# Spreading two gate rows to 128 partitions: diagonals and matmuls with ones, or a trip through memory

## What is computed

```python
mod = c_act @ w_mod[l] + b_mod[l]
sh1, sc1, g1, sh2, sc2, g2 = [m[:, None, :] for m in jnp.split(mod, 6, axis=-1)]
h = rms_norm_2(x, norm_attn[l]) * (1.0 + sc1) + sh1
qa, ka, va, qb, ckv, qi, ki, wi = jnp.split(h @ w_in[l], SPLIT_POINTS, axis=-1)
...
mix = jnp.concatenate([out_a, out_b], axis=-1) @ w_out[l]
x = x + g1 * mix
h = rms_norm_2(x, norm_ffn[l]) * (1.0 + sc2) + sh2
x = x + g2 * conv_ffn(h, w_up[l], conv_w[l], conv_b[l], w_down[l])
```

## Time and profile before

| | us |
|---|---|
| median of 3 runs | 2412.99 |
| lowest and highest | 2411.38, 2413.26 |
| profiled execution | 2410.21 |
| its span | 2408.5 |

### The profile page before, as it was taken

How to read it: one execution, slowest core, us unless ns; L and a number is a source line. 1 busy time by engine, 2 the same in 40 slices (tenths; PEclk the granted TensorE clock), 3 DMA queues, 4 the chain that set the end, 5 groups by cost and what they waited for, 6 DMA issues and landing times.

```text
span 2408.5 us, 29108 instructions
## 1 busy us (share of the span) xinstructions
PE 2294.6 (95%) x10764; PEld 1888.7 (78%) x10764; DVE 1672.4 (69%) x1848; ACT 991.6 (41%) x1009; POOL 133.3 (6%) x190
## 2 busy tenths in 40 slices
PE   8799998989999999999879999998999999999996
PEld 7688886878888878788668677877788888888885
DVE  6688787787776867767683556785466666666666
ACT  4543443433443334334333345434444444444442
POOL 2011000000000000000000000000000000000000
PEclk9899998999999999999988999999999999999998
DMA  8678675777877777777535444454555555555552
GB/s 290 233 260 271 228 265 188 256 268 250 289 237 255 274 248 264 258 259 273 199 108 134 149 117 132 140 181 156 175 185 185 188 192 186 181 190 191 181 189 101
DMA packets 261800, 501.28 MB, mean 208 GB/s; under 512 B 16753, under 2 KB 70289, under 8 KB 261104
## 3 DMA queue, kind: packets, MB, share of 16 engines
q1 hardware_dynamic: 230656, 382.39, 48.1%
q0 software_dynamic: 30800, 117.03, 14.0%
q10 hardware_dynamic: 288, 1.11, 0.1%
HBM read 496.80 MB, written 3.67 MB: 208 GB/s over the span
## 4 chain that ended last, share of the span: by engine, by line
PE 54%; issue 36%; DVE 4%; DMA 4%; ACT 2%; POOL 1%; SPq 0%; DVEq 0%; ACTq 0%; POOLq 0%
PE pair_t L399 15%; PE pair_t L401 15%; PE pair_t L400 15%; DMA raw<-in_attn_w_in_dram 1%; PE turn L507 1%; PE sc L1501 1%; DVE m_acc L980 1%; ACT w_hi L388 1%; DVE w_lo L393 1%; PE sc L737 1%; PE sc L514 1%; DMA raw<-in_ret_w_out_dram 1%; DMA raw<-in_w_in_dram 1%; PE sc L729 1%; PE turn L1509 0%
## 5 line engine op out<-in xcount | busy, mean ns | idle before, releaser
L393 DVE TENSOR_TENSOR w_lo<-raw,w_hi 128x2048 fp32r<-128x2048 f32 (+1 forms) x371 | 824.5, 2225 | 566.6 <-ACT w_hi L388 561.3
L388 ACT ACTIVATE w_hi<-raw 128x2048 fp32r<-128x2048 f32 (+1 forms) x371 | 690.9, 1864 | 1095.2 <-DMA raw<-in_ret_w_in_dram 367.0
L399 PE MATMUL pair_t<-w_hi,x_hi 128*128 128x512 f32 (+2 forms) x2112 | 825.0, 391 | 19.5 <-DVE w_lo L393 16.4
L401 PE MATMUL pair_t<-w_hi,x_lo 128*128 128x512 f32 (+2 forms) x2112 | 811.1, 384 | 0.0
L400 PE MATMUL pair_t<-w_lo,x_hi 128*128 128x512 f32 (+2 forms) x2112 | 810.6, 384 | 0.0
L399 PEld LDWEIGHTS pair_t<-w_hi,x_hi 128*128 128x128 f32 x2112 | 402.0, 190 | 106.2 <-DVE w_lo L393 17.8
L401 PEld LDWEIGHTS pair_t<-w_hi,x_lo 128*128 128x128 f32 x2112 | 401.6, 190 | 78.0
L400 PEld LDWEIGHTS pair_t<-w_lo,x_hi 128*128 128x128 f32 x2112 | 402.1, 190 | 73.7 <-issue 0.2
L980 DVE SCALAR_TENSOR_TENSOR m_acc<-m_raw,csilu,m_acc 128x1024 f32<-128x1024 f32 x180 | 230.7, 1281 | 4.3 <-DMA m_raw<-in_w_mod_dram 0.9
L399 PE MATMUL pair_t<-w_hi,f_hh 128*128 128x512 f32 x352 | 140.4, 399 | 6.9 <-DVE f_hl L2243 6.9
L401 PE MATMUL pair_t<-w_hi,f_hl 128*128 128x512 f32 x352 | 138.6, 394 | 0.0
(11 more groups left out here) (332 smaller groups left out, 2073.5 us busy)
## 6 DMA issues: line engine op xcount, KB each, us to landing
m_raw<-in_w_mod_dram POOLq DMA_DIRECT2D x96, 1024.0 KB, 6.9
raw<-in_ret_w_in_dram SPq DMA_DIRECT2D x192, 512.0 KB, 4.6
raw<-in_w_up_dram SPq DMA_DIRECT2D x176, 512.0 KB, 4.2
raw<-in_w_down_dram SPq DMA_DIRECT2D x88, 512.0 KB, 4.4
raw<-in_attn_w_in_dram SPq DMA_DIRECT2D x64, 512.0 KB, 4.6
raw<-in_ret_w_out_dram SPq DMA_DIRECT2D x64, 512.0 KB, 4.6
raw<-in_w_in_dram SPq DMA_DIRECT2D x56, 512.0 KB, 4.6
raw<-in_attn_w_out_dram SPq DMA_DIRECT2D x32, 512.0 KB, 4.9
```

The source lines that it names most:

```text
L388: act.activation(chunk(w_hi, c, width), chunk(raw, c, width), ACT.Copy).then_inc(sem("hi"), 1)
L393: v.tensor_tensor(chunk(w_lo, c, width), chunk(raw, c, width), chunk(w_hi, c, width).bitcast(F32), ALU.subtract).then_inc(sem("lo"), 1)
L399: pe.matmul(to, xh, wh, start=start, stop=False)
L401: return pe.matmul(to, xl, wh, start=False, stop=stop)
```

## The change

The 8 diagonals, the 32 matmuls with ones and the 8 copies go. After chunk 1 of block 1 PE transposes the 16 columns of g1 and the 16 of g2 into bank `sc[1]`: 16 partitions, 256 columns. DVE copies them to `gate_rows` after its second chunk of block 2. POOL writes them to a scratch tensor in memory, 2 x 2048 values, waits for the write, and issues two loads that read one row of 2048 values each and write it to all 128 partitions of `rows`. POOL does this behind the loads of `b_wuk` and `b_wuv`, ahead of the latent's power. DVE waits for `gate_out` ahead of the first head's scores, since `gate_rows` shares their buffer, and for `gate_in` ahead of the first sum. PE's wait for the eight copies becomes a wait for the one, a chunk later.

```diff
-        gate_diag = over("gate_diag", b_s_at, [2, 4, P], F32)
+        gate_rows = over("gate_rows", b_s_at, [2 * P], F32)
...
+        gates = nc.dram_tensor("gate_rows_kept", (2, D), F32, kind="Internal").ap()
...
-            def gates(c):
-                for b in range(2):
-                    n = 2 * c + b
-                    if n == 0:
-                        pe.wait_ge(sem("mod_read"), A_KV + R_HEADS)
-                    pe.wait_ge(sem("gate_diag"), n + 1)
-                    if n >= 2:
-                        pe.wait_ge(sem("gate_row"), n - 1)
-                    for m in range(4):
-                        mm = pe.matmul(sc[b][:, m * P:(m + 1) * P], ones[:, :], gate_diag[:, b, m, :],
-                                       start=True, stop=True)
-                    mm.then_inc(sem("gate_mm"), 1)
             def turn_qi0(c):
                 if c == 0:
                     pe.wait_ge(sem("i_q"), 1)
                     pe_turn_pairs(pe, i_q, "i_q_turned")
-                gates(c)
+                elif c == 1:
+                    pe.wait_ge(sem("mod_read"), A_KV + R_HEADS)
+                    for m in range(2):
+                        mm = pe.transpose(sc[1][0:KC, m * P:(m + 1) * P],
+                                          modc[:, (2 + 3 * m) * KC:(3 + 3 * m) * KC], ident[:, :])
+                    mm.then_inc(sem("gate_turned"), 1)
...
-                    pe.wait_ge(sem("gate_row"), 8)
...
+                    pe.wait_ge(sem("gate_copied"), 1)
...
-            act_blocks(act, B_B0 + 1, {0: [lambda: qi(0), lambda: qiT(0), lambda: gates(0)],
-                                       **{c: [lambda c=c: gates(c)] for c in (1, 2, 3)}})
+            act_blocks(act, B_B0 + 1, {0: [lambda: qi(0), lambda: qiT(0)]})
...
+            def gates_copied():
+                v.wait_ge(sem("gate_turned"), 1)
+                v.tensor_copy(gate_rows[0:KC, :], sc[1][0:KC, 0:2 * P]).then_inc(sem("gate_copied"), 1)
...
-            vec_blocks(v, B_B0 + 1, {0: [lambda: mod_read(v, A_KV + R_HEADS - 1), lambda: gates(0)],
-                                     1: [lambda: qiT(0), lambda: gates(1)],
-                                     2: [lambda: gates(2)], 3: [lambda: gates(3)]})
+            vec_blocks(v, B_B0 + 1, {0: [lambda: mod_read(v, A_KV + R_HEADS - 1)],
+                                     1: [lambda: qiT(0)], 2: [gates_copied]})
...
+                    if g == 0:
+                        v.wait_ge(sem("gate_out"), 16)
...
+                if t == 0 and c == 0:
+                    v.wait_ge(sem("gate_in"), 16 * 2)
...
+            g.wait_ge(sem("gate_copied"), 1)
+            get(bass.AP(tensor=gates.tensor, offset=gates.offset, ap=[[P, KC], [D, 2], [1, P]]),
+                gview(gate_rows[0:KC, :], 2), "gate_out")
+            g.wait_ge(sem("gate_out"), 16)
+            for m in range(2):
+                get(rows[:, m, :], broadcast_row(gates, m * D, D), "gate_in")
```

More of the change, by code:

```diff
@@ L1789, in done @@
                 act.wait_ge(sem("products"), CH * (B_B0 + b) + 4)
[L1791 to L1796, removed]
             act_blocks(act, B_B0, {})
```

## The result

| | before | changed |
|---|---|---|
| median, us | 2412.18 (4 launches) | 2397.61 (4 launches) |
| lowest and highest | 2410.98, 2413.26 | 2393.91, 2398.79 |
| profiled execution | 2410.21 | 2398.79 |
| ratio, 95% interval | | 0.9939, 0.9923 to 0.9956 |

What follows compares the result with a forecast made beforehand. PE's own order was taken to bound the kernel; savings after block 1's four chunks, 3.0 + 3.3 + 1.7 + 1.7 = 9.7 us, took the median from 2412.99 to 2403.3 us, range 2397.5 to 2407.2.

Steps and rivals of the forecast that it cites:

- The pieces: Gate matmuls after each of the four chunks of block 1, second attention; removing them saves PE 9.7 us net.
- The share of the waits: PE's idle time ahead of gate pieces in block 1, 2.6 us of the 9.7 forecast.
- The transposes: Two transposes with 128 columns added on PE after chunk 1 of block 1; taken as 0.3 us, no wait.
- ACT, DVE, POOL, the trip: Removed copies and diagonals give nothing beyond the waits; added DVE copy, POOL's write and two row loads cost 0.
- The cover: Rows' 2.1 MB beside blocks 2 and 3's loads: 8.9 us free against 6.5 needed; block 2's last small chunk ready in time.
- Block 2's clock: Block 2's 96 matmuls keep their two speeds, 17.58 us in all; bounds 10.8 and 20.5 us.
- The critical load: Last chunk of block 3, loaded once block 2 releases its buffer; moves with block 2's end and keeps its 5.40 us.
- The starting point: Median of the runs of the kernel before, 2412.99 us; runs spread over 1.9 us, 1 us allowed either way.
- B: Rival, 12%: clock stays high through block 2; 2398.5 us, or 2396.6 if no queue forms.
- B's second half: With block 2 fast, DMA becomes the bound, last landing at 1308.9; only 4.8 of the 6.7 us count.
- C: Rival, 12%: clock falls at block 2's first narrow matmul (2.9 us) or rows jam (2.2 us); 2406.2 us.
- D: Rival, 3%: row loads served slowly, wait after block 2 grows; slower by 4.8 us if both need 23.4 us.

Runs made afterwards that it cites:

- e6: Kernel before with block 2's matmuls 256 columns wide instead of 80; ratio 0.9978 against the kernel before.
- e2: Changed kernel with four bare pieces of 16 matmul records back after block 1's chunks, without diagonals and copies; 2407.20 us, ratio 0.9994 to the kernel before.
- e7: Changed kernel with all 64 bare matmul records in one go after chunk 0 of block 1; ratio 0.9986 to the kernel before.
- e3: Changed kernel without the write to memory and the two row loads, gates left out of the result; 2397.40 us, ratio 0.9952 to the kernel before.
- e4: Changed kernel with block 2's matmuls 256 columns wide instead of 80; 2398.10 us, ratio 0.9953 to the kernel before.
- b1: The kernel before again, no edit; ratio 0.9997, clock's fall 6.44 us into block 2, which took 14.76 us.
- e11: 32 rounds of growing wide, then narrow matmuls inserted between blocks 1 and 2, every second with a piece; falls 3.1 to 6.4 us without, 3.3 to 6.3 with.
- e8: Changed kernel with 64 more PE records in an idle stretch ahead of the second attention; 2397.75 us, ratio 0.9951 to the kernel before; critical load 5.43 us.
- e9: Changed kernel with 24 equal rounds inserted between blocks 1 and 2, every second with a piece; falls about 4.8 us without, 5.7 with.

## Why the prediction was right or wrong

**The pieces: right.** Forecast 9.7 us between the query turns and block 2. Measured 27.56 and 27.26 before (e6's 27.93 has a fall of the clock in it), 17.51 to 17.53 in six traces without pieces: 9.9. The share of the waits was right too (2.6 forecast less the transposes, 2.1 to 2.4 by e2 and e7). The transposes were covered by the 0.3 us set for them.

**ACT, DVE, POOL, the trip: right.** e2 shows that ACT's and DVE's part is worth nothing beyond the waits, e3 that the trip costs nothing in this kernel. The write landed in 2.5 us (3.3 forecast), the rows in 6.1 (bound 9.6). The last small chunk of block 2 was split at 1298.95 to 1299.44, beside the rows' traffic; PE reached it at about 1301.7. The cover held, with the clock falling as it did; e4 against e6 suggests 1.5 us of cost where it doesn't fall.

**Block 2's clock: the step that failed.** "I keep the two speeds" took the profiled execution's 17.58 us for a property of the kernel. It is one draw. The fall comes anywhere from 3.1 to 6.4 us after the first narrow matmul; the profile of before held nearly the earliest place, the profile after a late one (6.18). That is 2.86 of the 13.5 us between the two stretches. It needs neither the removal of the pieces nor any other edit: b1 has the late place in the kernel before. The bounds set for the block (10.8 and 20.5 us) did contain it, but the value was taken at one end of the real range, 17.6 of 14.6 to 17.6. A fall at 4.6 us, the mean of e11's 32 stretches, would give 96 x 0.213 - 4.6/0.112 x 0.101 = 16.3.

**The critical load: a term missing.** It was taken to keep its 5.40 us, as it hangs on the end of block 2. It did not, since the removed matmuls moved the instruction packet out of it. Six traces with the packet give 11.0 us from the end of block 2 to the keys, five without give 10.3 (e4, whose loads queue, left aside): 0.7 us of gain that no step had.

**The starting point.** The median of three launches, 2412.99, was taken as known to 1 us. Later launches of the same kernel ran from 2403.3 to 2418.6, with medians of 2409.4, 2411.1 and 2410.3. So about 2 us of the first 14.6 are most likely the luck of the first launches.

**Together** the change is worth 9.9 + 0.7 = 10.6 us by the traces, with the clock's place left the same in both. With the places as they fell, the two traces of before and the three of the changed kernel differ by 11.6 us on average in the stretch (54.76 against 43.11). The three comparisons of the changed kernel give 14.7, 12.5 and 12.3 us (0.9939, 0.9948, 0.9949 of 2410), e3 and e8 11.6 and 11.8. All five lie above 10.6; the intervals of all but the first reach well below it, and the first reaches it. One or two us above that sum stay open. A later fall by the change's timing, 16.2 against 15.2 us for block 2 in the few traces there are, would be 1 us of them, and it is not shown.

**The rivals.** B (the clock stays high) did not come. In all ten traces with 80 columns the clock fell while PE was fully busy. By the rule of the Trainium skill cited in the prediction ("TensorE: Matmul & The Clock Gate", Part 1) a stretch without idle keeps 2.4 GHz, and these ten traces disagree. e4 and e6 show the same 96 matmuls at nearly the same pace with the clock at 1.00 when they are 256 columns wide, so whether PE is busy by the profile does not decide it. B's second half, that DMA then becomes the bound, was right: e4's load queued and gave back 2.1 of the 3.2 to 4.3 us that its block 2 had gained. C and D did not come; the rows landed in less time than the nearest row had.

## What to carry to other kernels

Work on the engine that sets the end is paid in full, and can be summed from the starts in its timeline; check only that what follows hangs on its end and not on a clock of its own. Before a duration from one profile goes into such a sum, ask whether it depends on where something periodic or unrelated falls, like the clock's fall in a narrow stretch or an instruction load in a critical transfer: then its range belongs into the forecast, and a difference of two profiles is not the change's. A second profile of the same kernel, unchanged, shows this. Then ask also whether the change shifts the place at which the unrelated thing falls: two or three profiles of each kernel are needed to see that.

## What the runs showed of the hardware

- 96 back-to-back matmuls of 80 columns, with PE shown busy all the time, let the granted clock fall from 2.4 to 1.2 GHz, between 3.1 and 6.4 us after the first, in ten traces of the kernels and in all 32 stretches of e11; 256 columns at almost the same pace (0.12 us instead of 0.11) did not, in e4 and e6. The narrow ones take 0.213 us each on the slow clock.
- The place of the fall is not fixed by the narrow stretch: the same kernel had it at 3.3 and at 6.4 us (before, b1). Rounds of equal length lock to one place (e9), rounds of growing length sweep it (e11).
- A 16 KB packet of instructions in the stretch of a critical 1 MB load went with 5.15 to 5.91 us instead of 4.66 to 4.82. Adding 64 records to an idle stretch of PE, the last of them 83 us ahead of the load, was enough to bring it there (e8).
